# Heads in pairs in two attention mixers of a float32 kernel, with a reordered sliding-window mixer and padded up-projections

## What is computed

```python
merged = (gates[:, :, 0] * (o_fox @ w_up_fox[i])
          + gates[:, :, 1] * (o_sb @ w_up_sb[i])
          + gates[:, :, 2] * (o_dsa @ w_up_dsa[i]))
x = layer_norm(DEEPNORM_ALPHA * x + merged @ w_out[i], ln1_g[i], ln1_b[i])
ffn = jnp.square(jax.nn.relu(x @ w_ff_in[i])) @ w_ff_out[i]
ple = jax.nn.sigmoid(x @ w_ple_gate[i]) * (p[i] @ w_ple[i])
```

```python
s = einsum('bhqd,bhkd->bhqk', qn, kn) + einsum('bhqr,bkr->bhqk', qr, kr)       # MLA
s_w = einsum('bkgqd,bkjd->bkgqj', q_rot, k_b) * scale ; s_c = ctx_scores(q_pl)  # SWA
p_w, p_c, _ = joint_softmax(where(valid, s_w, NEG_INF), s_c, sink)
out = (pv(p_w, v_b) + pv(p_c, v_c)) @ w_o
```

## Time and profile before

| | us |
|---|---|
| median of 3 runs | 2934.86 (2931.61 to 2936.7) |
| the profiled execution, its own time | 2928.99 |
| its span | 2927.2 |
| PE busy | 2759.3 (94%) |
| PE weight loads busy | 2388.4 (82%) |
| DVE busy | 1572.0 (54%) |
| ACT busy | 1080.9 (37%) |
| PE's share of the chain that ended last | 81% |

### The profile page before, as it was taken

One profiled execution on the slowest core, in us unless ns is written; L12 is line 12 of the kernel. 1 busy time (PEld: TensorE's weight loads), 2 busy tenths in 40 slices (PEclk: granted clock), 3 DMA queues, 4 the chain that ended last, 5 costly groups with the idle time before them and its releaser, 6 DMA issues.

```text
span 2927.2 us, 44322 instructions
## 1 busy us (share of the span) xinstructions
PE 2759.3 (94%) x17920; PEld 2388.4 (82%) x17920; DVE 1572.0 (54%) x2309; ACT 1080.9 (37%) x1428; POOL 0.2 (0%) x4
## 2 busy tenths in 40 slices
PE   7999899999989969999989999999999999989997
PEld 6887899888779968887876688787887877967897
DVE  7676565678656564333375453333453433666665
ACT  3453453335445443222241433222232222345543
POOL 0000000000000000000000000000000000000000
PEclk9998999999899989999998999999999999989998
DMA  7645567565465734354432024444434445311563
GB/s 214 195 155 171 174 194 214 153 195 160 159 201 186 202 110 113 110 141 115 141 80 72 1 58 123 132 112 135 132 101 116 122 129 147 108 42 44 143 189 101
DMA packets 585240, 394.55 MB, mean 135 GB/s; under 512 B 43686, under 2 KB 579140, under 8 KB 584900
## 3 DMA queue, kind: packets, MB, share of 16 engines
q1 hardware_dynamic: 585028, 391.63, 46.1%
HBM read 390.54 MB, written 1.05 MB: 134 GB/s over the span
## 4 chain that ended last, share of the span: by engine, by line
PE 81%; DVE 10%; ACT 4%; DMA 2%; issue 2%; SPq 0%; DVEq 0%; ACTq 0%
PE bank L2015 81%; DVE w_lo L1190 3%; ACT w_hi L839 2%; DMA raw<-in_ffn_w_out 2%; DVE xs L1205 2%; DVE t L1205 1%; DVE h_lo L1205 0%; DVE t L1198 0%; DVE acc L1198 0%; DMA raw<-in_w_in 0%; ACT x_hi L843 0%; ACT xs L843 0%; ACT t L843 0%; DVE t L1202 0%; DMA bf<-in_b_forget 0%
## 5 line engine op out<-in xcount | busy, mean ns | idle before, releaser
L1190 DVE TENSOR_TENSOR w_lo<-raw,w_hi 128x2048 fp32r<-128x2048 f32 (+3 forms) x338 | 689.9, 2041 | 594.4 <-ACT w_hi L839 592.3
L839 ACT CAST w_hi<-raw 128x2048 fp32r<-128x2048 f32 (+3 forms) x338 | 574.8, 1701 | 803.4 <-PE bank L2015 419.2
L2015 PE MATMUL bank<-h_hi,w_hi 128*128 128x512 f32 (+1 forms) x1720 | 599.1, 348 | 23.2 <-DVE h_lo L1205 16.2
L2015 PE MATMUL bank<-h_lo,w_hi 128*128 128x512 f32 (+1 forms) x1720 | 591.9, 344 | 0.0
L2015 PE MATMUL bank<-h_hi,w_lo 128*128 128x512 f32 (+1 forms) x1720 | 591.1, 344 | 0.0
L2015 PE MATMUL bank<-x_hi,w_hi 128*128 128x256 f32 x1344 | 385.9, 287 | 33.2 <-DVE x_lo L1205 13.6
L2015 PEld LDWEIGHTS bank<-h_hi,w_hi 128*128 128x128 f32 x1720 | 326.1, 190 | 77.9 <-issue 20.9
L2015 PE MATMUL bank<-x_lo,w_hi 128*128 128x256 f32 x1344 | 377.7, 281 | 0.0
L2015 PE MATMUL bank<-x_hi,w_lo 128*128 128x256 f32 x1344 | 377.2, 281 | 0.0
L2015 PEld LDWEIGHTS bank<-h_hi,w_lo 128*128 128x128 f32 x1720 | 326.8, 190 | 39.0
L2015 PEld LDWEIGHTS bank<-h_lo,w_hi 128*128 128x128 f32 x1720 | 326.2, 190 | 37.5
(11 more groups left out here) (280 smaller groups left out, 3775.7 us busy)
## 6 DMA issues: line engine op xcount, KB each, us to landing
raw<-in_ffn_w_in SPq DMA_DIRECT2D x176, 512.0 KB
raw<-in_ffn_w_out SPq DMA_DIRECT2D x64, 704.0 KB
raw<-in_w_in SPq DMA_DIRECT2D x40, 1024.0 KB
xs<-in_mod_w SPq DMA_DIRECT2D x36, 1024.0 KB, 7.0
raw<-in_mod_w SPq DMA_DIRECT2D x36, 1024.0 KB
raw<-in_w_ff_in SPq DMA_DIRECT2D x32, 1024.0 KB
raw<-in_w_ff_out SPq DMA_DIRECT2D x32, 1024.0 KB
raw<-in_w_out SPq DMA_DIRECT2D x8, 1024.0 KB
```

Source lines behind the costliest of these rows:

```text
L839: act.copy(w_hi[s][:, w], raw[at % SLOTS][:, w]).then_inc(hi_made, c.did(hi_made))
L1190: dve.tensor_tensor(w_lo[s][:, w], raw[r][:, w], w_hi[s][:, w].bitcast(F32), ALU.subtract).then_inc(lo_made, c.did(lo_made))
L2015: ins = pe.transpose(o, l, r) if transpose else pe.matmul(o, l, r, start=start, stop=stop)
```

## The change

1. Up-projections of sb and dsa take 128 rows in the third block. The 64 added rows of `w` are zeros brought by one more DMA for each of these chunks, and those of `o_hi` and `o_lo` are set to zero once in each layer.
2. The ple chunk comes ahead of the four gate chunks. Its four products go to `rt`, `rv`, `rd`, `rd`; the first two stand ahead of the layer norm's `x_sum` product, the last two between that and the `sq` products. Four mod products move from behind chunks 36, 38, 42, 46 to behind 40, 42, 44, 47.
3. MLA takes units of two heads in pairs. PE computes two units' scores at once: both 128-row products, then the 64-row ones of the two heads in turn.
4. SWA pairs heads h and h + 4, so that one lies in the upper and one in the lower half. Scores of both alternate between row halves; both units' weighing alternates between column halves of one bank. The query and output weights are permuted to fit.
5. SWA has one key chunk (two tiles of four heads) in place of two. Order on PE: keys of the tokens, queries 0, keys of the context, queries 1 to 3 with the rotary products between them (on banks 0 and 1), then the values, the last two of whose four products stand behind the first scores.
6. Attention outputs rotate over three banks in place of two.

```diff
-        + [("out", c) for c in range(4)] + [("plegate", c) for c in range(4)] + [("ple", 0)]
+        + [("out", c) for c in range(4)] + [("ple", 0)] + [("plegate", c) for c in range(4)]
-MOD_AFTER = [6, 8, 10, 13, 16, 18, 20, 22, 24, 26, 28, 30, 32, 34, 36, 38, 42, 46]
+MOD_AFTER = [6, 8, 10, 13, 16, 18, 20, 22, 24, 26, 28, 30, 32, 34, 40, 42, 44, 47]
-MLA_UNITS = [(h, part) for h in range(MLA_H) for part in range(3)]
-SWA_UNITS = [(h, part) for h in range(SWA_H) for part in range(2)]
+MLA_UNITS = [(2 * j + half, part) for j in range(MLA_H // 2) for part in range(3) for half in range(2)]
+SWA_UNITS = [(SWA_HEAD[t, half], part) for t in range(SWA_H // 2) for part in range(2) for half in range(2)]
...
-                                rows = slice(0, HALF if b and k == 2 else P)
-                                product(d[:, S * t:S * t + S], [z[rows, k, cols] for z in w],
-                                        (o_hi[rows, b % 2, k, :], o_lo[rows, b % 2, k, :]), k == 0, k == 2,
+                                product(d[:, S * t:S * t + S], [z[:, k, cols] for z in w],
+                                        (o_hi[:, b % 2, k, :], o_lo[:, b % 2, k, :]), k == 0, k == 2,
...
+                ple(range(0, 2))
+                layer_norm_sums(lambda qs: ple(range(2, 4)) if qs[0] == 0 else None)
...
+                for s in range(n + 3):
+                    if s < n and s % 2 == 0:
+                        score([claim(rs4), claim(rs4)], units[s:s + 2])
+                    if meanwhile is not None:
+                        meanwhile(s)
...
+                    if paired:
+                        if s >= 4 and s % 2 == 0:
+                            pe.wait_ge(rt2.free, rt2.all_used())
+                            weigh([t2[:, 0, :], t2[:, 1, :]], units[s - 4:s - 2])
+                        if 2 <= s < n + 2:
+                            turn(s - 2)
...
-                front(1, 1, (0, 1), [[(rd, d_full)] * 2, [(ra, a_full)] * 2])
+                keys(wk, 0)
+                half_sum(1)
+                queries(0)
+                keys(wk, 1)
+                used_chunk(0)
+                flush()
+                used_chunk(1)
+                queries(1)
...
+                rotation([kd[:, j, 0:S] for j in range(2)], rs, s_full)
+                turn_queries(0)
...
+                values(0)
+                turn_queries(3)
+                values(1)
+                pe.wait_ge(roped, c.next(roped, 5))
...
+                    for b, t, g, hp, toks in both:
+                        mm(b[:, 0:S], q2rot[hp, t, toks], kd[hp, g, 0:S], True, True)
+                    for b, t, g, hp, toks in both:
+                        mm(b[:, S:2 * S], q2[hp, t, toks], kd[hp, g, S:2 * S], True, True, s_full)
...
+                    for k in range(4):
+                        for half, (wt, (h, _)) in enumerate(zip(wts, pair)):
+                            g = h // (SWA_H // SWA_KV)
+                            mm(ob[0][HALF * half:HALF * half + HALF, P * part:P * part + P], vw[:, k, DH * g:DH * g + DH],
```

More of the change, by code:

```diff
@@ L1447, in _ @@
                     projected(k)
+                    if k == 0:
+                        for part in (o_hi, o_lo):
+                            dve.memset(part[HALF:P, 1, 2, :].bitcast(F32), 0.0).then_inc(v_step, c.did(v_step))
                     m += 1
@@ L2646, in swa, with turn_queries @@
-                soft_attention(SWA_UNITS, score, weigh)
+                    copied[q] = rd.used
+                def turn_queries(q):
+                    pe.wait_ge(d_free, c.value(d_free, copied[q] + 1))
+                    rotation([q2[:, 2 * q + j, :] for j in range(2)], rs, s_full)
+                wk = parts(chunk(), KT, 256)
+                kb = [claim(ra) for _ in range(2)]
+                keys(wk, 0)
+                half_sum(1)
+                queries(0)
+                keys(wk, 1)
@@ L2647, in swa @@
+                soft_attention(SWA_UNITS, score, weigh, True, lambda s: values(s + 2) if s < 2 else None)
                 ok = x_tiles(ow_hi, ow_lo, KT)
```

309 lines of the change are left out of this document (168 added, 141 removed).

## The result

| | us |
|---|---|
| median before (4 runs beside it) | 2934.38 |
| median after (4 runs) | 2862.59 (2856.93 to 2866.78) |
| ratio | 0.9754, 95% interval 0.9735 to 0.9774 |
| the profiled execution of after | 2856.93, span 2855.1 |
| PE busy after | 2663.7 (93%) |

The forecast was 2859. The span fell by 72.1 us, and the forecast sum was 75.7. That the total agrees says little about its terms, so each is looked up on its own.

A forecast was written before the change was run, and what follows sets the result against it. PE was taken to bound the kernel (busy 94%, 81% of the chain). Gains 7.5 + 27.1 + 9.5 + 17.6 + 14 = 75.7 us off the profiled 2928.99 give 2853.3; the median's 5.9 more makes 2859, range 2832 to 2893.

The forecast's parts named there:

- SWA's attention: Paired units in SWA's attention: DVE bounds at 2.43 us a unit, 83.6 us where it was 91.1; gain 7.5.
- PE needs 1.62 of that ... so DVE should not wait: SWA's attention: PE needs 1.62 of DVE's 2.43 us a unit, so scores are ready in time for DVE.
- Rival (d): Slower: PE pauses in each pair, 1.2 GHz through both attentions; MLA loses 55 us, SWA 13; 2967 us; chance 0.03.
- SWA's front: Stretch up to SWA's first mask: 96 matmuls go, 48 value matmuls move behind the first scores; gain 27.1 us.
- The new wait: SWA's front: queries 1 come 5.8 us earlier, so PE waits 2.6 us for their w_lo.
- MLA: MLA's attention: pairs share 64-row time, 14.9 us, less 5.4 of waits for DVE; gain 9.5, ends 4 and 16.
- no wait, and more under the low clock: MLA's upper end, 16 us: PE never waits for DVE and more is gained at the stage's low-clock start.
- Up-projections: sb and dsa up-projections padded to 128 rows: 8.8 us a layer, 17.6 in two; ends 5.6 and 23.4.
- While the clock stayed low: Up stage: PE ran full blocks mixed with 64-row ones during the low clock, which rose at about 280.5, in out.
- since PE's idle time ahead of this stretch stays too: Up stage: reason given for expecting a short low-clock spell to stay, charged at 1.6 us.
- Rival (b): Up stage: clock returns on busy time alone, padding does nothing for it; 5.6 in place of 17.6, 2871 us; chance 0.15.
- Ple: Moving the ple chunk ahead of the gates removes a 10.6 us stretch; gain 7.0 us a layer, 14 in both.

The follow-up runs named there:

- the second trace: Another trace (span 2866.3 us) of the changed kernel, run once more unaltered; that run measured 2865.1 us, ratio 0.9765 to the kernel before.

## Why the prediction was right, and where not

**SWA's attention, 7.5 forecast, 4.2 and 3.6 measured** (9.2, and 5.9 and 5.3, by the right first mask; the prediction's "Before, that was 91.1 (2591.39" reads the second unit's mask as the first). The unit was right: 2.30 us by DVE and 2.84 with an `ow_lo`, as summed, and PE waits for DVE. The step that failed is "PE needs 1.62 of that ... so DVE should not wait". It left out what idle time does to PE's clock. In the first trace three steps take 3.62 in place of 2.84 us (2.3 in all); 0.8 more went at the start, where the third unit's scores stand behind 48 value matmuls, and 0.3 in the tail. In the second, one such step costs 0.7, the start 0.7, and the tail 2.6, partly at the low clock. Rival (d) had this mechanism, with a price of 13 us for the whole stage; it came in small. That the spells come with PE's idle time is shown by the runs in which PE waits less.

**SWA's front, 27.1 forecast, 24.6 and 23.5** (25.4, and 22.9 and 21.8, by the right first mask). From the first dense matmul at 2480.42 to the first mask at 2526.32 are 45.9 us, forecast 43.9. The new wait was named, but mis-sized: 3.26 in place of 2.6, because DVE's copy of queries 0 stands behind the `w_lo` and PE needs its bank:

```profile
2492.62 2.29 DVE L1205 TENSOR_TENSOR w_lo<-raw,w_hi 128x2048 fp32r<-128x2048 f32 x1 [1.30 <-ACT w_hi L853]
2494.95 0.69 DVE L1223 COPY q<-bank 128x512 f32<-128x512 f32 x1
```
```profile
2495.79 0.36 PE L2044 MATMUL bank<-h_hi,w_hi 128*128 128x256 f32 x1 [3.26 <-DVE q L1223]
```

After that wait the next 48 matmuls took 7.3 us and not 5.8, at the low clock for a part. Ahead of 2480.42 another 0.5 went.

**MLA, 9.5 forecast, 13.9 and 14.7.** Pairs take 6.34, 6.09 and 6.51 us, forecast 6.1 to 6.2; the wait for DVE is 0.53, 0.28 and 0.29, forecast 0.45. Twelve pairs gain 9.0. What was missing is the start: "no wait, and more under the low clock" stood at the upper end, and the rise some 5 us after the first score in place of 16 is worth the other 5. The later weighing confirms the wait's place and price, the single units both parts.

**Up-projections, 17.6 forecast, 13.8 and 18.5.** That padding raises the clock here is shown by two runs from either side (16.8 us in the trace, padding taken out of the kernel after; 19 in the medians, padding put into the kernel before). "While the clock stayed low" has only half of the mechanism: with padding the clock does not fall ahead of dsa in the first place. The short spell that I expected to stay "since PE's idle time ahead of this stretch stays too", at 1.6 us a layer, is not there. One of 3.4 us came 11 us later, behind PE's wait of 3.44, which follows from the DVE pace that I summed but whose effect on the clock I had not priced there. That DVE sets the pace was right, down to the `m_lo` that I put at 264.4 and that ends at 263.4. In the first trace layer 2 lost some 3 us to a low spell inside its attention script that the second trace has shorter. Rival (b) is out.

**Ple, 14 forecast, 13.6 and 12.8 over both layers**, 11.4 for the move alone: part of the stretch's gain is the padding's. The norm grew by 1.3 us (1.8 allowed). Behind it PE waits 1.54 us for the second gate chunk's `w_lo` (1.8 allowed):

```profile
320.51 0.38 PE L2044 MATMUL bank<-x_hi,w_hi 128*128 128x256 f32 x1 [1.54 <-DVE w_lo L1205]
```

**The sum.** Forecast and result agree within 4 us because a term too low (MLA, by 4 to 5) stands against two too high (SWA, by 6 to 8 together), and because stretches that I had at nothing moved by 1.9 us net in this trace. In the second trace they cost 12.2. That the median fell on the forecast is in part luck; that it lay in the range is not.

## What to carry to other kernels

Price a change on a half-filled array twice, once for the halves that now run together and once for the clock. In MLA it came back some 5 us after the first score with pairs, and after 14 to 16 us with single units. In the up stage it fell and stayed low for 24 us where one block in three had 64 rows, and did not fall there with padding. Padding with zeros can pay for itself. Before you take work off PE or DVE in a loop that three engines share, count every engine's cycle and the single buffers in it: here taking the mask (0.33 us of DVE a unit) off DVE bought nothing by itself, since PE with its single turning bank was as slow. With two banks and an early pair the stage was 3.4 us shorter than in the changed kernel, and with the masks behind the scores ACT was next. A gap that an improvement opens on PE is not free either, if the clock falls in it.

## What the runs showed that I had not expected

**Two paces of the same dense stream at full clock.** The windows of ffout in layer 1 in the two traces of one and the same kernel:

```profile
431.00:518.00 87.00, 87.00 (x770) 87.00 (x770) 43.92 (x32) 31.84 (x18) 0.00 (x0) 1.00 0.77 204
```
```profile
431.00:518.00 87.00, 87.00 (x741) 87.00 (x740) 42.44 (x31) 30.79 (x17) 0.00 (x0) 1.00 0.76 200
```

PE is busy throughout at a granted clock of 1.00 in both, yet one trace has 770 matmuls in 87 us and the other 741: 0.113 us each or 0.117. In the gate and ffin chunks of one trace the pace changes at each mod product, and once more without one (96 matmuls at 0.1134 us, then 96 at 0.1178, 144 at 0.1134, 144 at 0.1178, and all behind them at 0.1133), and the second trace has the same pieces with the paces exchanged. ffout alone is 86.9 or 90.3 us by this. That is the -3.4 and +3.4 in the balance, and it may be a good part of why runs of one kernel lie 10 us apart. I don't know the cause.

**A cost of the new ple place, 400 to 900 us further on.** In the feed-forward units ahead of MLA all eleven traces with the early ple show PE waits that no trace with the late one shows (the kernel before, padding alone, ple late): 1.7 and 2.4 us in the kernel after, ahead of the second half of a unit's down-projection. The chain leads to ACT's `w_hi` and the load of `ffn_w_out`. The program issues the same loads there at the same distances. With the late ple ACT begins on the chunk 7.2 us after its load was issued (1210.25 to 1217.42):

```profile
1217.42 1.37 ACT L853 CAST w_hi<-raw 128x1408 fp32r<-128x1408 f32 x1 [7.03 <-DMA raw<-in_ffn_w_out]
```

In the kernel after it begins 8.6 us behind (1197.98 to 1206.60), with the same DMA as the releaser. Why the transfer lands later is open; no run was made for it.

**Halves overlap without alternation.** Two heads' 64-row scores that the program issues one head after the other took the same 1.07 us as when they alternate; for 64-column weighing alternation was worth 0.5 us a pair.
